# Scatter one-hots built token by token with three 128-column instructions instead of four 1024-column ones

## The reference

```
def peer_layer(x, w_q, keys1, keys2, u_tab, v_tab):
    q = (xt @ w_q).reshape(T, 8, 2, 128)
    v1, i1 = top_k(q[:, :, 0] . keys1, 16)        # i1, i2 in 0..127
    v2, i2 = top_k(q[:, :, 1] . keys2, 16)
    sc, pos = top_k(v1 + v2 over all 256 pairs, 16)
    eidx = (i1 * 128 + i2)[pos]                   # 8 * 16 = 128 experts a token
    gate = softmax(sc)
    a = u_tab[eidx] . x                           # dot of each chosen expert with x
    w = gelu(a) * gate
    y = sum over the 128 chosen of w * v_tab[eidx]
```

## Time and the profile before

| what | value |
|---|---|
| median of 3 runs | 1473.58 us (1473.45 to 1474.05) |
| the profiled execution, its own time | 1473.52 us |
| its span, from first to last instruction | 1471.8 us |
| TensorE busy | 1446.8 us, 98% |
| VectorE busy | 1080.6 us, 73% |
| GpSimd busy | 995.9 us, 68% |
| ScalarE busy | 606.5 us, 41% |
| granted TensorE clock, mean | 0.998 |

### The profile page before, as it was taken

The page is one execution under the profiler, slowest core; times in us unless marked ns, Lnnn a source line. Parts: engine busy times, 40 slices in busy tenths (PEclk is TensorE's granted clock), DMA queues, the critical chain, the costliest instruction groups (busy, mean ns, idle before and its releaser), DMA issues.

```text
span 1471.8 us, 25054 instructions
## 1 busy us (share of the span) xinstructions
PE 1446.8 (98%) x8011; PEld 1285.8 (87%) x8011; DVE 1080.6 (73%) x2085; ACT 606.5 (41%) x1014; POOL 995.9 (68%) x613
## 2 busy tenths in 40 slices
PE   9999999999999999999999999999999999999997
PEld 5888777889999999999999999888888888888875
DVE  5466767688999989999999983755555555555587
ACT  5666741334333344444444443333333333333332
POOL 3332321335586758778887778888888888888886
PEclk9999999999999999999999999999999999999999
DMA  6212220323586868999999999999999999999981
GB/s 237 73 59 100 72 73 0 129 86 123 179 289 203 266 232 295 394 389 367 382 388 365 378 375 365 341 367 357 352 348 356 367 356 355 342 348 353 353 339 61
DMA packets 133574, 397.95 MB, mean 270 GB/s; under 512 B 12753, under 2 KB 55505, under 8 KB 131345
## 3 DMA queue, kind: packets, MB, share of 16 engines
q1 hardware_dynamic: 96064, 262.93, 50.2%
q0 software_dynamic: 37456, 134.37, 23.4%
HBM read 347.12 MB, written 50.14 MB: 270 GB/s over the span
## 4 chain that ended last, share of the span: by engine, by line
PE 91%; DVE 4%; ACT 2%; POOL 1%; issue 1%; DMA 0%; POOLq 0%; SPq 0%; ACTq 0%; DVEq 0%
PE banks L1598 16%; PE banks L1600 16%; PE banks L1599 16%; PE banks L1653 12%; PE banks L1654 12%; PE banks L1655 12%; PE banks L1715 2%; PE banks L1866 2%; PE banks L1867 1%; PE banks L1699 1%; PE banks L1807 1%; DVE probs L1100 1%; POOL lo L408 0%; POOL x L644 0%; DVE wgt_lo L1478 0%
## 5 line engine op out<-in xcount | busy, mean ns | idle before, releaser
L408 POOL TENSOR_TENSOR lo<-raw,hi 128x1024 fp32r<-128x1024 f32 x292 | 703.5, 2410 | 394.6 <-ACT hi L402 356.7
L1598 PE MATMUL banks<-x1T_hi,hi 128*128 128x384 f32 (+2 forms) x1168 | 401.2, 344 | 0.8 <-POOL lo L408 0.5
L1600 PE MATMUL banks<-x1T_hi,lo 128*128 128x384 f32 (+2 forms) x1168 | 395.8, 339 | 0.0
L1599 PE MATMUL banks<-x1T_lo,hi 128*128 128x384 f32 (+2 forms) x1168 | 395.6, 339 | 0.0
L402 ACT ACTIVATE hi<-raw 128x1024 fp32r<-128x1024 f32 x292 | 306.8, 1051 | 9.3 <-DMA raw<-u_t 4.7
L1653 PE MATMUL banks<-hi,wgt_hi 128*128 128x512 f32 x750 | 292.0, 389 | 1.8 <-DVE wgt_lo L1478 1.8
L1655 PE MATMUL banks<-hi,wgt_lo 128*128 128x512 f32 x750 | 291.8, 389 | 0.0
L1654 PE MATMUL banks<-lo,wgt_hi 128*128 128x512 f32 x750 | 291.8, 389 | 0.0
L1478 DVE TENSOR_TENSOR wgt_lo<-wgt,wgt_hi 128x384 fp32r<-128x384 f32 x125 | 79.3, 635 | 208.9 <-issue 110.4
L1598 PEld LDWEIGHTS banks<-x1T_hi,hi 128*128 128x128 f32 x1168 | 219.5, 188 | 5.2 <-issue 0.7
L1600 PEld LDWEIGHTS banks<-x1T_hi,lo 128*128 128x128 f32 x1168 | 219.4, 188 | 4.4
(11 more groups left out here) (203 smaller groups left out, 1814.6 us busy)
## 6 DMA issues: line engine op xcount, KB each, us to landing
raw<-u_t SPq DMA_DIRECT2D x128, 512.0 KB
raw<-v_tab SPq DMA_DIRECT2D x128, 512.0 KB
g_scratch<-stage SPq DMA_DIRECT2D x12, 2048.0 KB
gelu_scratch<-gelu SPq DMA_DIRECT2D x116, 192.0 KB
ga<-gelu_scratch SPq DMA_DIRECT2D x29, 768.0 KB
gg<-g_scratch SPq DMA_DIRECT2D x14, 1536.0 KB
raw<-w SPq DMA_DIRECT2D x26, 512.0 KB
raw<-w_pq SPq DMA_DIRECT2D x16, 512.0 KB
```

The source lines that it names most:

```text
L408: eng.tensor_tensor(l[:, :], raw[:, c % RAW_SLOTS, :], h[:, :].bitcast(F32), ALU.subtract).then_inc(lo_ready, 1)
L1598: pe.matmul(o, h[:, s], hiT[:, k, tokens], start=(k == 0), stop=False)
L1599: pe.matmul(o, h[:, s], loT[:, k, tokens], start=False, stop=False)
L1600: ins = pe.matmul(o, l[:, s], hiT[:, k, tokens], start=False, stop=(k == KT - 1))
```

## The change

Before, a group of 8 tokens takes four `tensor_tensor` instructions over 128 x 8 x 128 elements: compare the counting row 0..127 (f32, kept in PSUM) with i1, compare it with i2, multiply the first result with the high and with the low gate. After, each token takes three `tensor_scalar` instructions over 128x128: the counting row, now 16-bit numbers in PSUM, is compared with a scalar of each partition (i2), and, compared with i1, multiplied by a second scalar (the high or the low gate) in the same instruction. A scalar of each partition is a [128, 1] column in SBUF. The intermediate `is_i1` and its semaphore go. The gates in `gateT_hi` and `gateT_lo` move from PSUM to SBUF. The 16-bit counting row is written by VectorE into SBUF once (`iota_half`) and copied to PSUM by ScalarE as 64 words of 32 bits. The VectorE loop over the six double chunks is written out.

```
-        iota_home = banks[:, 6, 0:NKEY]
+        iota_words = banks[:, 6, 0:NKEY // 2]
+        iota_home = iota_words.bitcast(F16)
...
-        gateT_hi = banks[:, 6, NKEY:NKEY + DENSE]
-        gateT_lo = banks[:, 7, 0:DENSE]
+        gateT_hi = sb("gateT_hi", [P, DENSE], F32, scat)
+        gateT_lo = selT[:, 2, :]
...
-            act.activation(iota_home, iota[:, :], ACT.Copy).then_inc(homes_ready, 1)
+            act.wait_ge(iota_ready, 1)
+            act.activation(iota_words, small[:, P - NKEY // 2:P], ACT.Copy).then_inc(homes_ready, 1)
...
             turned_lo(TB - 1)
+            dve.tensor_copy(iota_half, iota[:, :]).then_inc(iota_ready, 1)
...
-                if not (isinstance(o, int) and o == 0 and tile == 0):
-                    dve.wait_ge(onehot_ready, 8 * o + tile)
-                t = bass.ds(2 * CHUNK * o + TOK_PER_TILE * tile, TOK_PER_TILE)
-                shape = [P, TOK_PER_TILE, NKEY]
-                row_of = iota_home.unsqueeze(1).to_broadcast(shape)
...
-                dve.tensor_tensor(is_i1[:, :, :], row_of, col(selT[:, 0, t]), ALU.is_equal).then_inc(is_i1_ready, 1)
-                dve.tensor_tensor(is_i2[slot][:, :, :], row_of, col(selT[:, 1, t]), ALU.is_equal)
-
-                dve.wait_ge(is_i1_ready, 8 * o + (tile + 1))
-                dve.tensor_tensor(gate_hi[slot][:, :, :], is_i1[:, :, :], col(gateT_hi[:, t]), ALU.mult)
-                dve.tensor_tensor(gate_lo[slot][:, :, :], is_i1[:, :, :], col(gateT_lo[:, t]),
-                                  ALU.mult).then_inc(onehot_ready, 1)
+                first_token = 2 * CHUNK * o + TOK_PER_TILE * tile
+                for k in range(TOK_PER_TILE):
+                    t = slice(first_token + k, first_token + k + 1)
+                    dve.tensor_scalar(is_i2[slot][:, k, :], iota_home, selT[:, 1, t], None, ALU.is_equal)
+                    dve.tensor_scalar(gate_hi[slot][:, k, :], iota_home, selT[:, 0, t], gateT_hi[:, t],
+                                      ALU.is_equal, ALU.mult)
+                    ins = dve.tensor_scalar(gate_lo[slot][:, k, :], iota_home, selT[:, 0, t], gateT_lo[:, t],
+                                            ALU.is_equal, ALU.mult)
+                ins.then_inc(onehot_ready, 1)
...
-            two_chunks(0, True)
-            with dve.Fori(1, O_MID - 1) as o:
-                two_chunks(o, False)
-            two_chunks(O_MID - 1, False, last=True)
+            for o in range(O_MID):
+                two_chunks(o, o == 0, last=o == O_MID - 1)
```

More of the change, by code:

```diff
@@ L196, in build @@
         rows = sb("rows", [P, ROWS, D])
-        dots8 = sb("dots8", [P, P])[:, 0:ROWS]
+        small = sb("small", [P, P])
+        dots8 = small[:, 0:ROWS]
+        iota_half = small[:, P - NKEY // 2:P].bitcast(F16)
         dots = sb("dots", [P, RANKS])
@@ L219, in hots @@
             return [sb(f"{name}{i}", [P, TOK_PER_TILE, NKEY], F16, scat) for i in range(slots)]
-        is_i1, = hots("is_i1_", 1)
         is_i2, gate_hi, gate_lo = (hots(name, HOT_SLOTS) for name in ("is_i2_", "gate_hi", "gate_lo"))
         gate_half = sb("gate_half", [P, DENSE], F16, scat)
+        gateT_hi = sb("gateT_hi", [P, DENSE], F32, scat)
+        gateT_lo = selT[:, 2, :]
         stage = [sb(f"stage{i}", [P, ETILES, CHUNK], F32, scat) for i in range(2)]
@@ L330, in build @@
         onehot_ready = sem("onehot_ready")
-        is_i1_ready = sem("is_i1_ready")
+        iota_ready = sem("iota_ready")
         scattered = sem("scattered")
@@ L1401, in _ @@
             dve.wait_ge(gate_step, 3)
-            dve.tensor_copy(gateT_hi, gate_half[:, :]).then_inc(gate_step, 1)
+            dve.tensor_copy(gateT_hi[:, :], gate_half[:, :]).then_inc(gate_step, 1)
             dve.wait_ge(gate_step, 4)
-            dve.tensor_tensor(gateT_lo, selT[:, 2, :], gateT_hi, ALU.subtract).then_inc(gate_step, 1)
+            dve.tensor_tensor(gateT_lo, gateT_lo, gateT_hi[:, :], ALU.subtract).then_inc(gate_step, 1)
             dve.wait_ge(gate_step, 5)
@@ L1412, in one_hots @@
                     dve.wait_ge(scattered, 16 * o + 2 * (tile - HOT_SLOTS + 1))
-                if not (isinstance(o, int) and o == 0 and tile == 0):
-                    dve.wait_ge(onehot_ready, 8 * o + tile)
-                t = bass.ds(2 * CHUNK * o + TOK_PER_TILE * tile, TOK_PER_TILE)
-                shape = [P, TOK_PER_TILE, NKEY]
-                row_of = iota_home.unsqueeze(1).to_broadcast(shape)
-                def col(ap):
-                    return ap.unsqueeze(2).to_broadcast(shape)
-                dve.tensor_tensor(is_i1[:, :, :], row_of, col(selT[:, 0, t]), ALU.is_equal).then_inc(is_i1_ready, 1)
-                dve.tensor_tensor(is_i2[slot][:, :, :], row_of, col(selT[:, 1, t]), ALU.is_equal)
-                dve.wait_ge(is_i1_ready, 8 * o + (tile + 1))
-                dve.tensor_tensor(gate_hi[slot][:, :, :], is_i1[:, :, :], col(gateT_hi[:, t]), ALU.mult)
-                dve.tensor_tensor(gate_lo[slot][:, :, :], is_i1[:, :, :], col(gateT_lo[:, t]),
-                                  ALU.mult).then_inc(onehot_ready, 1)
+                first_token = 2 * CHUNK * o + TOK_PER_TILE * tile
[7 more added lines that the diff above has]
+                ins.then_inc(onehot_ready, 1)
             one_hots(0, 0, True)
```

## The result

The changed kernel takes 1509.77 us (median of 5 runs, 1507.67 to 1511.19), the kernel before 1473.53 on the same chip: the ratio is 1.0242, with a 95% interval of 1.0231 to 1.0253. That is 36 us more, where 1518 us, or 44.5 more, were forecast. The profiled execution has a span of 1508.1 us, 36.3 more than before.

A forecast was written before the change was run, and what follows sets the result against it. TensorE was taken to bound the kernel, with VectorE slightly ahead in the middle stage; 1473.5 us + 58 for slower groups - 13.3 in hand = 1518 us, likeliest 1500 to 1540, 8-in-10 range 1472 to 1545.

The forecast's parts named there:

- The central step: VectorE, middle stage: small instructions start 0.199 us apart with one scalar, 0.259 with two; 717 ns a token.
- the half price of the columns: VectorE's small instructions: 128 columns at half of 1.04 ns each, 67 ns instead of 133.
- The term: VectorE, middle stage: a group takes 5.74 us against 4.53, +1.21 us a group, +58 us in 48 groups.
- the fixed part: VectorE's cost per instruction apart from columns: 68 ns without scalars, 132 with one, 192 with two.
- The margin: Middle stage: VectorE has 13.3 us in hand over TensorE at the end, gained at 0.27 us a group.
- The forecast's own sign: If the steps are right and TensorE waits less than 45 us, VectorE's lead over TensorE was misread.
- What TensorE would wait for: Middle stage: TensorE waits at the scatter for VectorE's gate_lo, some 45 us in all; GpSimd still gets its dots.
- Behind the stage: After the middle stage: nothing is given back, since TensorE is busy nearly throughout, and no further loss was forecast.
- No change: Rival: scalar fetches hidden behind the instruction before, mean step under 200 ns, time stays 1473.5 us; chance 0.17.
- Full price: Rival: VectorE's columns cost 66 ns more per instruction, group 7.32 us, time 1594 us; chance 0.15.
- Faster: Rival: a fast VectorE ends GpSimd's 32.7 us of waiting for dots; gain under 3 us; chance 0.03.

The follow-up runs named there:

- scalars_012: Changed kernel with is_i2 compared with a constant and gate_hi multiplied by 1.0, so instructions take none, one and two scalars of each partition (wrong results): 1473.65 us.
- row_f32: Changed kernel with the counting row in PSUM as 32-bit numbers again: 1585.23 us, ratio 1.0761.
- before_unrolled: Kernel before the change with only VectorE's loop over the double chunks written out: 1473.70 us, ratio 1.0000.
- split_first: Changed kernel, GpSimd in the middle stage splitting the expert tile before waiting for a free row buffer, its loop written out: 1505.66 us, ratio 1.0223.
- i2_by_group: Changed kernel with i2 compared for 8 tokens in one 1024-column instruction again, gates still token by token: 1491.55 us, ratio 1.0120.
- thin20: Changed kernel without the gate_lo instructions of 20 of the 48 groups, all after the first double chunk: 1479.78 us, ratio 1.0041.
- thin40: Changed kernel without the gate_lo instructions of 40 of the 48 groups, all after the first double chunk: 1480.06 us, ratio 1.0042.

## Why the prediction was right, and where it was off

**Steps of VectorE.** The central step held: one scalar 0.19 to 0.20 us, two 0.25, against 0.199 and 0.259 forecast; the token 0.697 against 0.717. scalars_012 shows the 60 ns of the first and of the second scalar by themselves, and row_f32 the half price of the columns. The term was over-sized by 0.16 us a group, 8 us in 48 groups: with 5.58 in place of 5.74 us the sum is +50 instead of +58. What was over-sized is the fixed part, 68 ns in the forecast and some 65 here (0.13 us without a scalar, less 67 ns for the columns), with steps of one and two scalars 7 ns shorter than forecast.

**The margin.** 50 less 13.3 is 37, where the stage lost 32.5; the missing 4 us fit the loop. The prediction said that writing it out saves nothing that shows. It does save VectorE time: in before_unrolled the last group is 4 us earlier than before the change (with its start 0.2 us later), as its experiment shows, and TensorE does not notice. In the changed kernel VectorE sets the pace, and 13.3 + 4.2 = 17.5 us were in hand: 50 - 17.5 is 32.5, what was measured. So an over-sized group and an under-sized margin add up: 8 and 4 us make the 12 by which the stage was forecast too long (44.6 against 32.5). The total is off by only 8, because 3.8 us are lost behind the stage, where the forecast had none; that part is luck. The forecast's own sign, steps right and TensorE waiting less than 45 us, pointed at a misread margin, and a third of the difference was that.

**What TensorE would wait for.** Here the prediction was wrong in a step: it put the wait at the scatter, for `gate_lo`, 45 us in all, and said that the dots are ahead of the scatter in VectorE's order, so that GpSimd would not be felt. In the changed kernel GpSimd, which asks for a free row buffer *before* it splits a tile, waits for the dots and hands their lateness on to the next expert tile: 24.9 us there, 0.3 us at the scatter (1.2 for the weight loads). split_first moves the wait back to where it was expected, with the stage as long. So the waiting instruction was named wrongly, and the price did not depend on it: both roads start at the same late VectorE.

**Behind the stage.** The prediction had nothing given back and nothing lost there. 3.8 us are lost in the profiled execution. TensorE waits once in the 12 tiles behind the stage, and in order of time ScalarE and TensorE show this:

```profile
949.55 1.06 ACT L404 ACTIVATE hi<-raw 128x1024 fp32r<-128x1024 f32 x1 [7.16 <-DMA raw<-u_t]
950.51 0.47 ACT L928 ACTIVATE kept<-banks 128x384 f32<-128x384 f32 x1
...
951.03 0.44 PE L1593 MATMUL banks<-x1T_hi,hi 128*128 128x384 f32 x1 [2.32 <-ACT kept L928]
```

ScalarE waits 7.16 us for a tile of `u_t`, and the gelu that it would do next, whose bank TensorE needs, is queued behind that wait. The granted clock has two levels, 2.4 and 1.2 GHz. Over these stretches its mean is below 1.00, so for a part of them it was at the lower one:

```profile
950.00:955.00 5.00, 3.97 (x16) 3.97 (x17) 2.47 (x5) 2.88 (x5) 4.03 (x4) 0.73 1.05 391
955.00:960.00 5.00, 5.00 (x28) 5.00 (x27) 2.14 (x5) 2.03 (x3) 4.52 (x4) 0.93 1.08 329
```

2.3 us of waiting and 5 x 0.27 + 5 x 0.07 = 1.7 us of clock are 4.0 us, about the 3.8. i2_by_group, which loses 4.2 us behind its stage, has the same wait for `kept` there, 3.0 us long. With split_first TensorE has only 0.5 us of gaps from 915 to 1045 us and the clock stays at 1.00, and 3.4 us come back. How much is lost here differs between executions: the five runs of the changed kernel lie 3.5 us apart, those of the kernel before 0.6, and one of the five of split_first took 1510.17. Why the tile came late is argued, not shown: the transfers are busy for all of that stretch (share 0.99 to 1.08), and the rows and tiles that GpSimd held back fall due there together.

**The rivals.** *No change* put the point of decision at 200 ns an instruction or 4.81 us a group; with 17.5 us in hand it would be 4.89. The runs bracket both: scalars_012 with 4.6 us stays at 1473.65, i2_by_group with 5.17 does not. But such a point holds only for a VectorE that is evenly slower. thin20 and thin40 are fast enough on the whole and still end at 1480, since the largest lateness up to any group counts. *Full price* is what row_f32 ran, 1585 us. *Faster* did not occur, and in thin40 a faster VectorE had nothing to gain behind the first double chunk: it waited 22.3 us for slots, and the time was that of thin20. The clock, which the forecast read as 1.00 in all its stretches, was 0.99 in the last of them; nothing in the sum hangs on that.

## What to carry to other kernels

Cost small instructions by the distance between starts, not by durations or columns: here a `tensor_scalar` of 128 16-bit columns was some 65 ns fixed, 60 for each scalar of a partition and 67 for the columns, so that going from one instruction to eight small ones bought half-price columns and lost more than that in fixed parts and scalars. Before an engine is changed that runs beside a full one, work out by how much it leads and how that lead grows; what counts is the largest lateness up to any point, since here the full engine did not make good what it had once lost. And a resource's lateness can reach the bound by another road than the direct one: who waits there is read after the fact, the price can be worked out before.

## What the runs showed of the hardware

A `tensor_scalar` with a 16-bit source in PSUM and a 16-bit destination in SBUF takes 0.52 ns a column, half of what the 32-bit row took (row_f32). The Trainium skill's page "VectorE: DVE Perf Modes" (section "Why PSUM operands drop a tier") leaves a PSUM source at most the mode with two packed 16-bit values per read, and the rate measured here is that of two columns at a time. The same page's formula for operations out of PSUM (section on the trn2 errata) gives, as an estimate, (120 + 64) / 0.96 = 192 ns for these. The measured steps agree with one scalar (0.19 us) and differ with none and two (0.13 and 0.25 us); by the formula the time would not have changed, and it did.

In row_f32 TensorE was busy for 374.6 of 451 us in the stage, and the granted clock of that stretch is 0.95 on average:

```profile
540.00:991.00 451.00, 374.57 (x2462) 356.94 (x2460) 450.62 (x1347) 150.71 (x238) 254.38 (x173) 0.95 0.73 269
```

In the changed kernel, where TensorE was busy for 350 of 375 us, it stayed at 1.00 in the stage and fell behind it, after the wait of 2.32 us. In row_f32 VectorE sets the pace, so that a slower TensorE inside the stage need not have cost anything; this was not tried by itself.
